# A two-part, two-layer transformer on one core: x and the embeddings are also loaded with features on the partitions, the first unit of weights is two, and TensorE multiplies zeros during the first loads

## The reference, cut to what matters

```python
h = rms_norm(x, attn_norm_g[l])
proj = h @ w_in[l]                     # latent attention, grouped attention, pooling, gates
merged = gates[0]*(o_mla @ w_a) + gates[1]*(o_gqa @ w_b) + gates[2]*(o_pool @ w_c)
x = x + merged @ w_out[l]
u = depthwise_conv(rms_norm(x, ffn_norm_g[l]) @ ffn_w_up[l])
x = x + (silu(u_gate) * u_val) @ ffn_w_down[l]
```

## Time and profile before

| | us |
|---|---|
| median of 3 runs (lowest, highest) | 1518.96 (1518.64, 1520.56) |
| the profiled execution, its own time | 1518.41 |
| its span in the profile | 1516.6 |
| mean granted clock of TensorE | 0.998 |
| TensorE busy | 1493.7 |
| VectorE busy | 1045.1 |
| ScalarE busy | 839.7 |
| GpSimd busy | 58.2 |
| DMA, mean over the span | 169 GB/s |

### The profile page before, as it was taken

One profiled execution on the slowest core, in us unless ns is written; L12 is line 12 of the kernel. 1 busy time (PEld: TensorE's weight loads), 2 busy tenths in 40 slices (PEclk: granted clock), 3 DMA queues, 4 the chain that ended last, 5 costly groups with the idle time before them and its releaser, 6 DMA issues.

```text
span 1516.6 us, 23950 instructions
## 1 busy us (share of the span) xinstructions
PE 1493.7 (98%) x9872; PEld 1347.6 (89%) x9872; DVE 1045.1 (69%) x1549; ACT 839.7 (55%) x1243; POOL 58.2 (4%) x70
## 2 busy tenths in 40 slices
PE   8999999999999999999999999999999999999998
PEld 7999979998899989799989977998888888899886
DVE  6897668776578877687855567655467556766446
ACT  5555557655446555665643476554456455655434
POOL 1110000000021000000000000000000000100000
PEclk9999999999999999999999999999999999999999
DMA  7643445565655434556566533655647543555562
GB/s 257 194 140 112 140 153 181 188 200 186 190 160 169 137 106 146 181 175 197 169 197 210 176 97 112 214 182 194 194 154 235 154 127 126 174 169 192 195 194 70
DMA packets 73565, 255.75 MB, mean 169 GB/s; under 512 B 8432, under 2 KB 10096, under 8 KB 73456
## 3 DMA queue, kind: packets, MB, share of 16 engines
q1 hardware_dynamic: 73168, 254.05, 51.8%
q10 hardware_dynamic: 288, 0.17, 0.1%
HBM read 253.14 MB, written 1.05 MB: 168 GB/s over the span
## 4 chain that ended last, share of the span: by engine, by line
PE 93%; DVE 3%; ACT 2%; DMA 1%; issue 1%; SPq 0%; POOL 0%; ACTq 0%; DVEq 0%
PE psum L1111 14%; PE psum L1113 14%; PE psum L1114 14%; PE psum L1120 14%; PE psum L1124 14%; PE psum L1122 14%; PE psum L1069 4%; PE psum L1270 2%; DVE w_low L1965 1%; PE psum L1355 1%; PE psum L1300 1%; ACT w_high L1515 1%; PE psum L1397 1%; DMA w_raw<-in_weights 1%; PE psum L1436 0%
## 5 line engine op out<-in xcount | busy, mean ns | idle before, releaser
L1965 DVE TENSOR_TENSOR w_low<-w_raw,w_high 128x1024 fp32r<-128x1024 f32 (+2 forms) x480 | 570.4, 1203 | 251.4 <-ACT w_high L1515 250.2
L1515 ACT ACTIVATE w_high<-w_raw 128x1024 fp32r<-128x1024 f32 (+2 forms) x480 | 495.4, 1042 | 308.1 <-PE psum L1124 166.5
L1111 PE MATMUL psum<-x_high,w_high 128*128 128x256 f32 x1504 | 430.1, 286 | 0.0
L1113 PE MATMUL psum<-x_low,w_high 128*128 128x256 f32 x1504 | 425.5, 283 | 0.0
L1114 PE MATMUL psum<-x_high,w_low 128*128 128x256 f32 x1504 | 425.4, 283 | 0.0
L1111 PEld LDWEIGHTS psum<-x_high,w_high 128*128 128x128 f32 x1504 | 288.4, 192 | 5.3 <-issue 4.6
L1113 PEld LDWEIGHTS psum<-x_low,w_high 128*128 128x128 f32 x1504 | 288.5, 192 | 0.4
L1114 PEld LDWEIGHTS psum<-x_high,w_low 128*128 128x128 f32 x1504 | 288.4, 192 | 0.0
L1120 PE MATMUL psum<-w_high,ff_high 128*128 128x512 f32 x256 | 100.0, 391 | 0.0
L1122 PE MATMUL psum<-w_low,ff_high 128*128 128x512 f32 x256 | 99.6, 389 | 0.0
L1124 PE MATMUL psum<-w_high,ff_low 128*128 128x512 f32 x256 | 99.6, 389 | 0.0
(11 more groups left out here) (264 smaller groups left out, 2397.4 us busy)
## 6 DMA issues: line engine op xcount, KB each, us to landing
w_raw<-in_weights SPq DMA_DIRECT2D x450, 512.0 KB, 4.1
w_raw<-in_weights SPq DMA_DIRECT2D x16, 384.0 KB, 3.1
w_raw<-in_weights SPq DMA_DIRECT2D x8, 416.0 KB, 4.8
rows<-in_second_rows SPq DMA_DIRECT2D x4, 512.0 KB, 4.9
w_raw<-in_weights SPq DMA_DIRECT2D x6, 256.0 KB, 2.7
out<-residual SPq DMA_DIRECT2D x2, 512.0 KB, 2.8
dil_masks<-in_consts SPq DMA_DIRECT2D x1, 576.0 KB, 5.7
residual<-in_x SPq DMA_DIRECT2D x2, 256.0 KB, 4.3
```

The costliest lines, as they stand in the source:

```text
L1111: eng.matmul(o, wh[:, j, cut], high[:, k, :], start=k == 0 and f % 2 == 0, stop=False, skip_group_check=True)
L1113: eng.matmul(o, wh[:, j, cut], low[:, k, :], start=False, stop=False, skip_group_check=True)
L1515: act(self.unit_view(self.wh, u), raw, ACT.Copy).then_inc(sem("w_high"), 1)
L1965: tt(self.unit_view(self.wl, u), raw, self.unit_view(self.wh, u), ALU.subtract).then_inc(sem("w_low"), 1)
```

## The change

Each part as it stands in the diff: x is also put into memory turned (`x_turned`, features on the partitions), and the embeddings only turned. At the start SyncE loads x_turned in three pieces (tiles 0 and 1, 2 and 3, 4 to 7) between the first units; x by tokens follows in two halves behind unit 2. `arrive` becomes a step of ScalarE and VectorE alone, which read the turned x straight from SBUF (in the scratch area) and split it. The first two k tiles are units of their own, so panel 0 has five units (1, 1, 2, 2, 2 k tiles) and the kernel 481. ScalarE issues the gains first and the identity second. TensorE starts with three matmuls of a tile that VectorE has filled with zeros. The squares move behind units 3 and 4. The embeddings need no transposes. Some semaphores are joined: identity with constants, pool weights with rows.

```diff
@@ weight_units
-            for k0 in range(0, kts, step):
-                own.append(dict(..., k0=k0, nk=min(step, kts - k0)))
+            first = [0, 1] if not units and not own else []
+            for k0 in first + list(range(len(first), kts, step)):
+                nk = 1 if k0 in first else min(step, kts - k0)
+                own.append(dict(..., k0=k0, nk=nk))
@@ Plan.arrive
-        add("turn", g, 0)
-        add("split", 0)
-        self.n_split = 1
-        add("turn", g, 1)
-        self.after(1, second)                 # turn 2, turn 3, square 0, mean
-        self.after(2, lambda: (add("square", g, 1), add("rstd", g)))
-        self.after(3, lambda: add("constants"))
+        for j in range(2):
+            add("arrive", j)
+            add("split", j)
+        self.n_split = 2
+        add("arrive", 2)
+        self.after(1, lambda: add("arrive", 3))
+        self.after(3, lambda: (add("square", g, 0), add("mean", g)))
+        self.after(4, lambda: (add("square", g, 1), add("rstd", g)))
+        self.after(4, lambda: add("constants"))
@@ memory
+        self.arriving = by_tile(self.scr[:, 0:DK * SEQ])
-                emb = by_token(sb(f"ple_tokens_{l}", TT * PLE, F32, ctx))
+                emb = by_tile(sb(f"ple_turned_{l}", PLE // P * SEQ, F32, ctx))
@@ sync
                 if n == 0:
-                    eng.dma_start(self.x[:, :, 2 * P:PANEL], src[:, :, 2 * P:PANEL]).then_inc(sem("x_loaded0"), 16)
+                    self.load_arriving(eng, 2, 4)
                 elif n == 1:
-                    eng.dma_start(self.x[:, :, PANEL:D], src[:, :, PANEL:D]).then_inc(sem("x_loaded1"), 16)
-                elif n == 3:
+                    self.load_arriving(eng, 4, DK)
+                elif n == 2:
+                    for half in range(2):
+                        c = slice(half * PANEL, (half + 1) * PANEL)
+                        eng.dma_start(self.x[:, :, c], src[:, :, c]).then_inc(sem(f"x_loaded{half}"), 16)
+                elif n == RAW_SLOTS - 1:
                     eng.dma_start(self.consts[:, P:N_HELD], dram["consts"][:, P:N_HELD]).then_inc(sem("consts_loaded"), 16)
             elif kind == "load_first":
-                eng.dma_start(self.x[:, :, 0:2 * P], src[:, :, 0:2 * P]).then_inc(sem("x_begun"), 16)
+                self.load_arriving(eng, 0, 2)
...
+    def load_arriving(self, eng, first, last):
+        eng.dma_start(self.arriving[:, first:last, :],
+                      self.dram["x_turned"][:, first * SEQ:last * SEQ].rearrange("p (k s) -> p k s", s=SEQ)
+                      ).then_inc(self.sem(f"x_arrived{first}"), 16)
@@ tensor
-        q.wait_ge(sem("ident_loaded"), 16)
+        q.wait_ge(sem("dve_step"), 1)
+        for n in range(3):
+            eng.matmul(bank[7], self.junk[1][:, 0:P], self.junk[1], start=True, stop=True)
...
-            elif kind == "emb":               # four transposes into bank 6
...
@@ scalar
-        eng.dma_start(self.consts[:, 0:P], self.dram["consts"][:, 0:P]).then_inc(sem("ident_loaded"), 16)
         eng.dma_start(self.cols[:, 0:N_FIRST_COLS], self.dram["first_cols"][0]).then_inc(sem("first_loaded"), 16)
+        eng.dma_start(self.consts[:, 0:P], self.dram["consts"][:, 0:P]).then_inc(sem("consts_loaded"), 16)
...
+            elif kind == "arrive":
+                j, = key
+                gain = self.gain(STAGE_MIX[0])
+                q.wait_ge(sem(("x_arrived0", "x_arrived2", "x_arrived4", "x_arrived4")[j]), 16)
+                for k in (2 * j, 2 * j + 1):
+                    act(self.features[STAGE_MIX[0]][0][:, k, :], self.arriving[:, k, :], ACT.Copy, scale=gain[:, k:k + 1]
+                        ).then_inc(sem("arrived_high"), 1)
...
             elif kind == "emb":
-                for i in range(2):
-                    d = act(self.ff[l][2][0][:, i, :], bank[6][:, i * SEQ:(i + 1) * SEQ], ACT.Copy)
+                q.wait_ge(sem("emb_loaded"), 16 * (l + 1))
+                act(self.ff[l][2][0], self.ff[l][1], ACT.Copy).then_inc(sem("emb_high"), 1)
@@ vector
+        q.step(eng.memset(self.junk[1], 0.0))
         q.wait_ge(sem("first_loaded"), 16)
...
+            elif kind == "arrive":
+                j, = key
+                gain, (high, low) = self.gain(STAGE_MIX[0]), self.features[STAGE_MIX[0]]
+                for k in (2 * j, 2 * j + 1):
+                    q.wait_ge(sem("arrived_high"), k + 1)
+                    d = stt(low[:, k, :], self.arriving[:, k, :], gain[:, k:k + 1], high[:, k, :], ALU.mult,
+                            ALU.subtract)
+                d.then_inc(sem("arrived_low"), 1)
...
                 if at(*step) > 1:             # square
                     q.wait_ge(sem("squared_odd"), at(*step) - 1)
+                else:
+                    q.wait_ge(sem("w_used"), 1)
...
-                    d = stt(low[:, i, :], bank[6][:, i * SEQ:(i + 1) * SEQ], 1.0, high[:, i, :], ALU.mult, ALU.subtract)
+                tt(low, self.ff[l][1], high, ALU.subtract).then_inc(sem("emb_low"), 1)
```

More of the change, by code:

```diff
@@ L114, in weight_units @@
             step = max(1, min(kts, UNIT // w))
-            for k0 in range(0, kts, step):
-                own.append(dict(name=name, layer=layer, source=source, panel=n, cols=cols, w=w, k0=k0,
-                                nk=min(step, kts - k0)))
+            first = [0, 1] if not units and not own else []
+            for k0 in first + list(range(len(first), kts, step)):
+                nk = 1 if k0 in first else min(step, kts - k0)
+                own.append(dict(name=name, layer=layer, source=source, panel=n, cols=cols, w=w, k0=k0, nk=nk))
         if name in BY_HALVES:
@@ L1024, in operand_ready @@
         name, l, sem, at = u["name"], u["layer"], self.sem, self.at
-        if name in ("proj", "gates_early", "gates"):
+        if name in ("proj", "gates_early", "gates") and l == 0:
+            q.wait_ge(sem("arrived_low"), k // 2 + 1)
+        elif name in ("proj", "gates_early", "gates"):
             q.wait_ge(sem("features_low"), at("turn", STAGE_MIX[l], k // 2))
@@ L1168, in tensor @@
                 b = TURN_BANKS[j]
[L1169 to L1173, removed]
+                self.x_ready(q, g, j // 2)
                 acquire(b)
@@ L1319, in tensor @@
                 free[2 * slot_of(name, l, half) + t] = (sem("y_added"), at(*step))
-            elif kind == "emb":
[L1322 to L1325, removed]
-                for i in range(2):
[L1327 to L1330, removed]
             elif kind == "sb_a":
@@ L1798, in scalar @@
                 l, = key
-                q.wait_ge(sem("emb_turned"), at(*step))
-                for i in range(2):
-                    d = act(self.ff[l][2][0][:, i, :], bank[6][:, i * SEQ:(i + 1) * SEQ], ACT.Copy)
-                d.then_inc(sem("emb_high"), 1)
+                q.wait_ge(sem("emb_loaded"), 16 * (l + 1))
+                act(self.ff[l][2][0], self.ff[l][1], ACT.Copy).then_inc(sem("emb_high"), 1)
             elif kind == "take_up":
@@ L2378, in vector @@
                 q.wait_ge(sem("emb_high"), at(*step))
-                for i in range(2):
-                    d = stt(low[:, i, :], bank[6][:, i * SEQ:(i + 1) * SEQ], 1.0, high[:, i, :], ALU.mult, ALU.subtract)
-                d.then_inc(sem("emb_low"), 1)
+                tt(low, self.ff[l][1], high, ALU.subtract).then_inc(sem("emb_low"), 1)
             elif kind == "take_gate":
@@ L2670, in pack @@
     arrays = {
[L2671 removed]
+        "weights": flat, "x": f["x"][0], "x_turned": f["x"][0].T.reshape(DK, P, SEQ).transpose(1, 0, 2).reshape(P, DK * SEQ), "first_cols": first_cols, "first_rows": first_rows,
         "pool_w": f["pool_w"].transpose(0, 2, 1, 3).reshape(DEPTH, P, POOL_G * P), "second_cols": second_cols,
[L2673 removed]
+        "second_rows": second_rows, "ple": f["p_2"][:, 0].transpose(0, 2, 1), "positions": f["positions_2"].reshape(TT, P).T,
         "consts": constants(),
```

23 lines of the change are left out of this document (7 added, 16 removed).

## The result

The changed kernel takes 1524.15 us (median of 7 runs, 1523.32 to 1524.73) against 1518.96 before (7 runs, 1518.64 to 1520.56): ratio 1.0032, 95% interval 1.0022 to 1.0042. Forecast were 1517.3 and a range up to 1520.0, so the time lies outside it, on the other side. The profiled execution took 1524.15 with a span of 1522.3, 5.7 more than before.

A forecast was written before the change was run, and what follows sets the result against it. TensorE was taken as the bound, busy 1493.7 of 1516.6 us. 0.8 us from the start and 0.9 from the embeddings made 1.7 off: profiled 1518.41 to 1516.7, median 1517.3, range 1514.5 to 1520.0.

The forecast's parts named there:

- Part 3: Behind panel 0: unit 5 ready just ahead of 19.6, rstd some 5 us later, nothing reaches TensorE, no cost.
- Part 2: Four later units of panel 0: held by VectorE and transfers, panel 0 ends at 19.6 against 20.36, 0.8 us gained.
- the mark of before: End of panel 0 in the kernel before, 20.36; whatever it gains, the kernel's end was said to gain.
- estimate at 436 GB/s: Transfers at the start: at 436 GB/s from 8.5 on, unit 4 would be released 0.5 us sooner than by the curve.
- The zeros: Three multiplications of zeros at TensorE's start: worth nearly nothing, over by 6.7 at the latest, delaying the first unit 0 to 0.3.
- Part 1: Start up to the first weight matmul: gains taken in at 4.9, first unit of weights starts at 6.9, not 8.64.
- Part 4: Embeddings: four transposes per layer go, twice, 0.44 us each, 0.88 us in all on TensorE's stream.
- C: Rival: extra megabyte at 304 GB/s, unit 4 released after 17.0, panel 0 1.1 us later, 1519.2 or 1520.9; chance 0.12.
- B: Rival: clock behind the two 3.1 us waits; neither drops it 1515.6, both do 1519.0; chance 0.20.
- A: Rival: transfers no bound, TensorE goes through from 6.9 to about 16.1, 4.3 + 0.9 off, 1513.8; chance 0.13.
- signs in the prediction's last line: Forecast wrong if panel 0 ends outside 18.5 to 20.4, or unit 5 is late and a wait appears behind 19.6.
- The prediction's other figure for them: Gains at the start: with ScalarE's and SyncE's queues on the same 16 engines, no earlier than 5.8, first matmul at 7.8.

The follow-up runs named there:

- e2: The changed kernel with diag and the row product of layer 0 five units later (after 9 and 11 units): 1519.81 us, ratio 1.0002.
- e9: The changed kernel with only the row product of layer 0 a unit later (after 7 instead of 6): 1519.80 us, ratio 1.0005.
- e1: The changed kernel with the squares of x after unit 0 and rstd after unit 1: 1520.51 us, ratio 1.0007.
- e12: The changed kernel with the first unit uncut, so four units in panel 0 as before: 1522.73 us, ratio 1.0026.
- e8: The kernel before with only the squares of x later, after 3 and 4 units instead of 1 and 2: 1520.68 us, ratio 1.0010.
- e4: e2 with x by tokens loaded behind unit 5 instead of unit 2: 1519.75 us, ratio 1.0000.
- e11: The kernel before with the turned embeddings alone: 1517.72 us, ratio 0.9995.
- e3: e1 without the three products of zeros at the start: 1520.39 us, ratio 1.0006.
- e5: e1 with the row product and diag of layer 0 one unit later: 1522.15 us, ratio 1.0015.
- e6: e4 with diag after 6 and row after 9, plus a product of zeros behind units 0 and 1 each: 1518.47 us, ratio 0.9993.
- e10: The changed kernel with token x, constants and rows loaded later, squares early, diag, row and tables moved, zeros behind units 0 and 1: 1517.93 us, ratio 0.9990.

## Why the prediction was wrong, point by point

- **The step that failed is Part 3**, "nothing reaches TensorE". It said rightly that rstd would come later (some 5 us; it was 6.4, 27.5 against 21.1) and followed it to ScalarE's take of panel 0, which was harmless (e2). It did not follow it to `diag` on VectorE and `row` on TensorE, which use the same rstd and whose place is set by a count of units. In the kernel before these two had 0.2 us of room (25.63 and 25.84), in the same timelines that the prediction draws on, but it names neither row and put the term at nothing. Cost: 3.64 us and 1.7 at half clock. Shown by e9: this one place, moved by one unit, gives 4.35 us back.
- **The count.** The cut of the first unit makes five units of panel 0; every `after(n)` of layer 0 moved one unit of 2.75 us forward on TensorE. The prediction counted five units, but not what hangs on the count. The late rstd and the count act together: with early squares alone 0.96 us of wait stay (e1), with the old count alone 2.43 (e12), with late squares alone 0.58 (e8, and there TensorE was late by itself). Even the start as forecast would have met this: with panel 0 over at 19.6, TensorE is at the row at 22.4 (an estimate: 19.6 + 2.75), and the diagonal came at 25.15 even in the kernel before, with rstd ready at 21.1.
- **Part 2, panel 0's end**, forecast 19.6, was 21.64. The reason was right in kind (units 3 and 4 come late with the token copy of x ahead of them; in e4, with it behind unit 5, ScalarE began on unit 4 at 15.0, earlier than in any of the six profiles with the order of the change), the size was not: the lag between the count of bytes and the release was taken as 0.75 from one unit of before and came out as 1.75 for unit 3 and 2.4 for unit 4 on the same curve. The rate was not at fault: 405, 377 and 399 GB/s in the stretches from 8.6 to 12.5, 15.9 and 17.2. By 17.2 some 5.5 MB had been moved, where the count puts the end of unit 4 at 4.59: about 0.9 MB of transfers issued later had been moved before unit 4 was released. Whether they went ahead of its bytes or its release came late behind them is not shown. These landings scatter by up to 1.6 us between executions, more than the whole gain that I had forecast for the start. And the mark of before, 20.36, is one draw as well: with the same start, e11 and e8 end panel 0 at 19.86 and 21.55, depending on when the slow spacing of the matmuls ends. The prediction's estimate at 436 GB/s is off by its own numbers: 2.42 MB take 5.6 us, which is 0.7 us sooner than the curve, not 0.5.
- **The zeros** were called worth nearly nothing: right for the change (e3). What was missed is that the clock can fall again behind them, in the gaps of units 0 and 1: half clock at 12.5 in the changed kernel, at 12.0 in e5, at 11.7 for 6.8 us in e4. With zeros in the gaps (e6) panel 0 ended at 19.32 and not at 21.99. But the clock does not always fall there: e9 has 1.77 us of work from 8.6 to 12.1 and e1 1.56, and both keep it. So the comparison of e4 with e6 is one of single profiles, and that the zeros always hold the clock is not shown; e6's ten runs have 0.996 to 0.998, none 0.995.
- **Part 1** held within 0.3: gains taken up at 5.10 (4.9), w_low of unit 0 ready at 7.1 (6.9), zeros over at 6.36 (at the latest 6.7; in e2, e9 and e10 it was 6.93). **Part 4** held: no transposes at 1047 and 1408, 0.46 and 0.52 less in the two stretches (0.44 each).
- **The rivals.** C (slower by the extra megabyte) named the transfers and unit 4's release after 17.0 as the turning point; it was 17.24, and panel 0 did end later than before by 1.28 (forecast there: 1.1). That the numbers agree is luck: C's reason was a queue at 304 GB/s, and it moved 405 and 377; and the 1.28 are a fifth of the loss. B's clock did fall, but not where B had it: behind the two long waits it is as before, full at 229.1 and 0.54 for 3.5 us at 630.0. A was wrong: the DMA share stayed at 1.0. No rival had a new wait on TensorE behind panel 0. Of the signs in the prediction's last line, the first came true (panel 0 ended outside 18.5 to 20.4), and of the second the half that counts: a new wait behind 19.6, though unit 5 was not late.
- Not settled: why unit 4's release scatters between executions, why the clock falls behind the gaps of units 0 and 1 in some and not in others, and where between 20 and 62 us VectorE would have to be relieved so that an early start isn't given back at the heads. This was seen (e6, e10), not tried further.

## What to carry to other kernels

When a change delays a value, list every step on every engine that reads it, and for each the time at which its engine arrives there and the room that it had before; the harmful reader here was a step of 0.5 us on the bounding engine. Where steps are placed by a count of work items, a change of the items' size is a change of every such place: hold the order of all queues before and after against each other before pricing anything. A shorter start is worth only what the next just-in-time meeting of TensorE and VectorE lets through: in e10, 2.0 us at 18 became 1.0 at 221 (221.34 against 222.35, the ends of the first long wait).

## What the runs showed that I had not expected

- The clock fell not only behind idle times of 3 us but behind a stretch with much work in it: 1.47 of 3.9 us (after) and 1.81 of 3.5 us (e4), each followed by the level of 0.5; in e4 it stayed there through 6.23 busy of 6.8 us. The gaps were 0.8 to 1.4 us each. The Trainium skill, TensorE: Matmul & The Clock Gate, section on the HAM clock gate, says that activity releases the throttle; its advice is put as one against long idle gaps, but it also tells of a kernel whose clock swings by short idle times between groups of matmuls. These two traces agree with that; e1 and e9, with like gaps, don't show it.
- The two waits of 3.15 us are followed by a half clock at one of their places in some executions (before, after and e2, at the second; e4, e10 and e11, at the first) and at both in others (e1, e5, e12). Mostly it costs 1.7 us; in e3 and e4 the clock stays at half for some 6 us and costs 2.9 and 3.1. One more at 1.7 fits the distance of the two groups in the times of the kernel before, and their mean granted clocks: beside e1 to e4 it is 0.998 in all 15 runs of the faster group and in one of the other, 0.997 in the remaining 15. No profile of that kernel's slower group was taken, so this is not shown.
- The gains, issued first, were taken up at 5.10 instead of 5.83. The prediction's other figure for them, no earlier than 5.8, did not come about; but unit 0's transfer, which runs beside them, is also half as large now, and no run separates the two.
